# One block instead of separate stages: layers 2 and 3 of a three-layer decoder kernel, with parts of the out-projection, the next norm and the final rows put elsewhere

## Chip, cores and metric

One NeuronCore of one Trainium2 chip runs the whole kernel. The metric is the device time of one execution in microseconds (us); the figure for a kernel is the median of its runs. Engines: TensorE (PE), VectorE (DVE), ScalarE (ACT), GpSimd (POOL), and SyncE (SP), which here only issues DMAs.

## What is computed

256 tokens of width 1024 pass three layers in fp32. Layer 1 (RWKV, latent attention and 32 experts) is the same in both kernels. Layers 2 and 3 are, cut to what matters:

```python
for layer in range(2):
    h = rmsnorm(x, norm_mix[layer])
    if layer % 2 == 0:                       # "even": layer 2 of the kernel
        y = h @ ev_w_in                      # 1024 x 3048
        o_a = dsa_mixer(...)                 # 8 heads; keys picked per query: lax.top_k(score, 64)
        o_b = diff_mixer(...)                # 4 heads, two softmaxes each, a = p0 - lam * p1
        mix = concatenate([o_a, o_b]) @ ev_w_out
    else:                                    # "odd": layer 3 of the kernel
        y = h @ od_w_in                      # 1024 x 2608
        # nsa_mixer: compressed keys and values gelu(flat @ w1) @ w2, selected and windowed attention, gates
        mix = nsa_mixer(...) @ od_w_out
    x = x + mix
    x = x + (silu(g @ w_gate) * (g @ w_up)) @ w_down      # g = rmsnorm(x, norm_ffn[layer]), width 2816
return rmsnorm(x, norm_final)
```

## The kernel before

Rows of tokens lie in two row blocks of 128 (TT = 2), the width in 8 chunks of 128 (KC = 8). To keep fp32 accuracy, most matrix products are three fp16 products (high by high, low by high, high by low): ACT makes the high part of a weight tile (a copy to fp16), DVE the low part (what the copy left), and PE multiplies.

Layers 2 and 3 are six stages, each an `nc.Block` of its own. At a block's end every engine waits for all others. Inside a block each engine runs its own program in the order in which it is written, with semaphores between them:

- `even_in`: norm of x on DVE, 16 transposes (L341), the in-projection in 12 tiles of up to 256 columns (L358), and beside it rope, the index scores of the 8 picking heads, and `take_eight` eight times on DVE (L2906, L2907: the 8 largest scores of each row are found and struck out), then L2951 and L2952, which turn the struck-out scores into the mask `ev_chosen`.
- `even_attention`: 8 units, the four differential ones first. Of a unit, PE makes the scores (L3186 to L3202, for units 4 to 7 with the mask), DVE `smallest` (L3112, the smallest score of each row, since scores are negated), ACT the exponentials, DVE `weigh` (L3119 to L3129), PE the transposes (L3214), DVE and ACT a copy each, PE the product with the values (L3228, L3235).
- `out_swiglu` (L418), used by both layers: 96 products of 512 columns of the out-projection (L692; 48 for each row block), norm and transposes (L699) of the rows, then 11 blocks of the feed-forward part, each 96 products of 256 columns up (L723) and 24 of 512 columns down (L732), with the weights streamed by SP.
- `odd_in` (L3282): the norm of x once more, 16 transposes (L341), 10 tiles of in-projection (L358). Beside it POOL clears four tiles and issues five loads: `emb` (L3321), `w1s` in two loads of 1 MB (L3323) and `w2s` (L3324, L3325). PE transposes `emb` after tile 1 (L3450) once all five have landed. After tile 3 come 32 fp32 products of 65 columns (L3463), the compression.
- `sparse_attention`: 16 units of the same build, then `out_swiglu` again, with the final norm. Its last part: DVE adds the last products to x (L659), ACT squares, DVE makes the sum and the reciprocal (L665 to L667), ACT the root, DVE one product over the whole row block (L673), SP writes out 512 KB for each row block (L495).

Between layers 2 and 3 there is in addition the exit of `Held` (L176, L177), which sets semaphores back and joins all engines. PSUM and SBUF of a stage are freed at its end.

## Time and profile before

| | us |
|---|---|
| median of three runs | 1129.85 |
| the runs | 1123.79, 1129.85, 1134.23 |
| the profiled execution, of which the trace is | 1124.25 |
| its span, first to last instruction | 1122.1 |

| engine | busy us | share of the span | instructions |
|---|---|---|---|
| PE | 985.7 | 88% | 8661 |
| PE weight loads | 708.9 | 63% | 8661 |
| DVE | 596.0 | 53% | 958 |
| ACT | 470.7 | 42% | 795 |
| POOL | 104.6 | 9% | 111 |

Where the stages lie: layer 1 ends near 440; `even_in` to 526; `even_attention` to 568; its `out_swiglu` to 768; `odd_in` to 848; `sparse_attention` to 915; the last `out_swiglu` to the end. The granted clock of PE is given as a share of its full 2.4 GHz; 0.5 is the lower level of 1.2 GHz. A row of the timeline is: start, duration, engine, line, operation, what is written and read, how many instructions in a row, and in brackets the idle time before it with what ended it. A PE row's duration is that of the whole run of instructions.

### The profile page before, as it was taken

How to read it: one execution, taken by the hardware profiler on the slowest of the kernel's cores; microseconds unless marked ns; L12 is line 12 of the kernel's file. 1: busy time of each engine (PE TensorE's matmuls, PEld its weight loads, DVE VectorE, ACT ScalarE, POOL GpSimd, SP SyncE). 2: the span in 40 equal slices, each digit the busy share in tenths (PEclk: the TensorE clock that was granted, in tenths of full speed). 3: DMA queues.
4: the chain of work that ended last, by engine and by line, in shares of the span. 5: the costliest groups of instructions: out<-in, count | busy, mean ns of one | idle time of the engine just before them, and what ended most of it. 6: DMA issues, size and time to landing. Idle time of an engine off the chain costs nothing. (4 is left out here: it accounts for less than half of the span.)

```text
span 1122.1 us, 20430 instructions
## 1 busy us (share of the span) xinstructions
PE 985.7 (88%) x8661; PEld 708.9 (63%) x8661; DVE 596.0 (53%) x958; ACT 470.7 (42%) x795; POOL 104.6 (9%) x111
## 2 busy tenths in 40 slices
PE   6998899789666677997889999997998889999996
PEld 5675787445333343885548777774886547777773
DVE  5667588431000004798764554536886864645543
ACT  6456552310000004663555455424665655534532
POOL 3410360000000001025000000002040000000000
PEclk9999898889888999998899999998998999999998
DMA  8723005999999996662062755634842033666520
GB/s 279 242 89 128 2 3 201 423 397 420 421 421 421 421 414 226 230 224 94 21 225 77 249 183 179 211 112 133 265 139 76 1 118 128 225 224 222 187 77 38
DMA packets 108453, 228.58 MB, mean 204 GB/s; under 512 B 7273, under 2 KB 86171, under 8 KB 93787
## 3 DMA queue, kind: packets, MB, share of 16 engines
q1 hardware_dynamic: 105403, 219.38, 53.9%
q0 software_dynamic: 2976, 8.14, 2.5%
q8 instruction: 54, 0.88, 0.3%
q14 instruction: 20, 0.16, 0.0%
HBM read 224.63 MB, written 1.05 MB: 201 GB/s over the span
## 5 line engine op out<-in xcount | busy, mean ns | idle before, releaser
L584 DVE SCALAR_TENSOR_TENSOR ffn_wu_lo<-ffn_w_up,ffn_wu_hi 128x2048 f16<-128x2048 f32 x40 | 90.0, 2288 | 32.6 <-ACT ffn_wu_hi L500 32.4
L1180 PE MATMUL rw_pB<-ring,kept 128*32 128x256 f32 x864 | 71.9, 430 | 27.5 <-DMA ring<-in_w_up 21.3
L723 PE MATMUL ffn_pG<-ffn_hT_hi,ffn_wu_lo 128*128 128x256 f16 x320 | 87.2, 273 | 0.0
L723 PE MATMUL ffn_pG<-ffn_hT_hi,ffn_wu_hi 128*128 128x256 f16 x320 | 87.2, 273 | 0.0
L723 PE MATMUL ffn_pG<-ffn_hT_lo,ffn_wu_hi 128*128 128x256 f16 x320 | 87.2, 273 | 0.0
L723 PE MATMUL ffn_pU<-ffn_hT_hi,ffn_wu_hi 128*128 128x256 f16 x320 | 87.2, 273 | 0.0
L723 PE MATMUL ffn_pU<-ffn_hT_lo,ffn_wu_hi 128*128 128x256 f16 x320 | 87.2, 273 | 0.0
L723 PE MATMUL ffn_pU<-ffn_hT_hi,ffn_wu_lo 128*128 128x256 f16 x320 | 87.2, 273 | 0.0
L500 ACT ACTIVATE ffn_wu_hi<-ffn_w_up 128x2048 f16<-128x2048 f32 x40 | 74.2, 1900 | 13.5 <-DMA ffn_w_up<-in_ffn_w_up 9.0
L601 DVE SCALAR_TENSOR_TENSOR ffn_hidden<-ffn_pU,ffn_gated 128x512 f32<-128x512 f32 x22 | 15.2, 690 | 111.2 <-ACT ffn_gated L518 111.2
L1180 PEld LDWEIGHTS rw_pB<-ring,kept 128*32 128x32 f32 x864 | 38.9, 124 | 54.3 <-issue 41.8
L1113 DVE TENSOR_TENSOR rw_mu_a<-rw_pB,rw_mu_a 128x256 f32<-128x256 f32 x8 | 3.4, 424 | 129.0 <-PE rw_pB L1180 129.0
L271 DVE SCALAR_TENSOR_TENSOR in_w_lo<-wt,in_w_hi 128x2048 f16<-128x2048 f32 (+2 forms) x22 | 53.5, 2433 | 17.0 <-ACT in_w_hi L264 16.9
L584 DVE SCALAR_TENSOR_TENSOR ffn_wd_lo<-ffn_w_down,ffn_wd_hi 128x2048 f16<-128x2048 f32 x22 | 50.4, 2292 | 22.1 <-ACT ffn_wd_hi L500 22.1
L518 ACT ACTIVATE ffn_gated<-ffn_pG 128x512 f32<-128x512 f32 x22 | 13.1, 597 | 114.6 <-PE ffn_pU L723 114.5
L732 PE MATMUL ffn_pY<-ffn_wd_hi,ffn_h_hi 128*128 128x512 f16 x176 | 53.7, 379 | 0.6 <-DVE ffn_h_lo L584 0.6
L732 PE MATMUL ffn_pY<-ffn_wd_hi,ffn_h_lo 128*128 128x512 f16 x176 | 53.7, 379 | 0.0
L732 PE MATMUL ffn_pY<-ffn_wd_lo,ffn_h_hi 128*128 128x512 f16 x176 | 53.6, 379 | 0.0
L358 PE MATMUL in_pY<-in_w_hi,in_sT_hi 128*128 128x256 f16 (+2 forms) x352 | 44.6, 275 | 1.0 <-ACT in_sT_hi L297 0.3
L264 ACT ACTIVATE in_w_hi<-wt 128x2048 f16<-128x2048 f32 (+2 forms) x22 | 42.1, 1915 | 4.8 <-DMA wt<-in_ev_w_in 2.2
L358 PE MATMUL in_pY<-in_w_lo,in_sT_hi 128*128 128x256 f16 (+2 forms) x352 | 42.2, 273 | 1.1 <-DVE in_w_lo L271 1.1
L358 PE MATMUL in_pY<-in_w_hi,in_sT_lo 128*128 128x256 f16 (+2 forms) x352 | 42.7, 273 | 0.3
(660 smaller groups left out, 2183.4 us busy)
## 6 DMA issues: line engine op xcount, KB each, us to landing
ring<-in_w_gate SPq DMA_DIRECT2D x27, 1024.0 KB, 26.1
ring<-in_w_up SPq DMA_DIRECT2D x27, 1024.0 KB, 26.7
ring<-in_w_down SPq DMA_DIRECT2D x24, 1024.0 KB, 26.2
ffn_w_down<-in_ffn_w_down SPq DMA_DIRECT2D x22, 1024.0 KB, 5.0
ffn_w_up<-in_ffn_w_gate SPq DMA_DIRECT2D x20, 1024.0 KB, 7.6
ffn_w_up<-in_ffn_w_up SPq DMA_DIRECT2D x20, 1024.0 KB, 9.9
wt<-in_ev_w_in SPq DMA_DIRECT2D x9, 1024.0 KB, 5.6
wt<-in_od_w_in SPq DMA_DIRECT2D x9, 1024.0 KB, 6.4
```

The source lines that it names most:

```text
L264: self.nc.scalar.activation(self.w_hi[:, k % 2, :, 0:n], self.wt[:, k % 2, :, 0:n], ACT.Copy, scale=W_SCALE).then_inc(self.hi_ready, 1)
L271: self.nc.vector.scalar_tensor_tensor(self.w_lo[:, k % 2, :, 0:n], self.wt[:, k % 2, :, 0:n], W_SCALE, self.w_hi[:, k % 2, :, 0:n], ALU.mu ...
L358: ins = self.nc.tensor.matmul(self.pY[:, slot, t, 0:n], x[:, c, t * P:(t + 1) * P], w[:, slot, c, 0:n], start=(term == 0 and c == 0), stop ...
L500: copy = lambda o, i, scale=1.0: nc.scalar.activation(o, i, ACT.Copy, scale=scale)
L518: nc.scalar.activation(gated[:, s, :], pG[:, s, :], ACT.Silu, scale=1.0 / W_SCALE).then_inc(silu_done, 1)
L584: return nc.vector.scalar_tensor_tensor(out, whole, scale, hi, ALU.mult, ALU.subtract)
L601: nc.vector.scalar_tensor_tensor(into, pU[:, s, :], 1.0 / W_SCALE, gated[:, s, :], ALU.mult, ALU.mult).then_inc(hidden_ready, 1)
L723: ins = T.matmul(p[:, s, j * SEQ:(j + 1) * SEQ], w[:, s, m, c, j::NJ], h[:, c, :], start=(n == 0), stop=(n == 3 * KC - 1))
L732: return T.matmul(pY[:, t, half * 512:(half + 1) * 512], h[:, s, at:at + P], w[:, s, j, half * 512:(half + 1) * 512], start=False, stop=st ...
L1113: nc.vector.tensor_tensor(hidden[:], pU[:, 0:D_EXPERT], gated[:], ALU.mult).then_inc(hidden_ready, 1)
L1180: ins = nc.tensor.matmul(into[i * CAP:(i + 1) * CAP, 0:D_EXPERT], h[:, c, i * CAP:(i + 1) * CAP], held[:, c * D_EXPERT:(c + 1) * D_EXPERT] ...
```

## The change

Layer 1 stays. For layers 2 and 3 one SBUF tensor (`field`) and one PSUM tensor (`later_pB`) are cut by hand into the stages' tiles, so stages can overlap. Four stages (in-projection, attention, feed-forward, next in-projection) run in one block without a barrier between them, and the other two in a second one; the exit of `Held` now stands between `odd_in` and `sparse_attention`.

```diff
+                with nc.Block(no_gpsimd_drain=True) as block:
+                    @block.tensor
+                    def _(pe):
+                        in2.tensor(pe)
+                        ea.tensor(pe)
+                        ffn2.tensor(pe)
+                        in3.tensor(pe)
...
+            with Held(nc) as held, ExitStack() as ctx3:
...
+                    @block.tensor
+                    def _(pe):
+                        nsa.tensor(pe)
+                        ffn3.tensor(pe)
```

**Picking.** Three of the eight `take_eight` and the making of the mask go from the end of `even_in` into DVE's program of the attention, and PE waits for the mask before the first unit that needs it.

```diff
+EIGHTS = {8: 2, 9: 2, 10: 1, 11: 0}
...
         smallest(0)
+        take_eight(pick)
...
         smallest(1)
+        take_eight(pick)
         weigh(0)
...
             left(u)
+            if u == 0:
+                take_eight(pick)
+                choose(pick).then_inc(picked, 1)
+            if u in LATE_LOWS:
+                out.low_part(dve, LATE_LOWS[u])
...
         for u in range(units):
+            if u + 2 == 4:
+                pe.wait_ge(picked, 1)
```

DVE at the start of layer 2's attention, before (`ei_` and `ev_` are tiles of `even_in`, `ea_` those of the attention):

```order
L2951 TENSOR_SCALAR ei_score<-ei_score 128x384
L2952 TENSOR_TENSOR ev_chosen<-ei_score,con_causal 128x384
L2799 UNCONDITIONAL_BRANCH
L3103 UNCONDITIONAL_BRANCH
L3145 TENSOR_TENSOR ea_prod<-ev_lam 128x128
L3146 TENSOR_REDUCE ea_s<-ea_prod 128x2
L3112 TENSOR_REDUCE ea_low_max<-ea_pS 128x2 x2
L3149 TENSOR_TENSOR ea_neg<-ea_s 128x1
```

and now, where L3006 and L3007 are a `take_eight` and L3310 is `smallest`:

```order
L3343 TENSOR_TENSOR ea_prod<-field 128x128
L3344 TENSOR_REDUCE ea_s<-ea_prod 128x2
L3310 TENSOR_REDUCE ea_low_max<-later_pB 128x2 x2
L3006 MAX field<-field 128x8
L3007 MATCH_REPLACE field<-field 128x128
L3006 MAX field<-field 128x8
L3007 MATCH_REPLACE field<-field 128x256
L3349 TENSOR_TENSOR ea_neg<-ea_s 128x1
```

The branches at the block's end are gone, and the rounds stand behind the `smallest` of units 0 and 1 and the `left` of unit 0.

**Out-projection.** The 48 products of one row block are issued chunk by chunk from the attention's last units on, each chunk once its low part is there.

```diff
+        def project(c):
+            pe.wait_ge(low_out, min(c, units // 2) + 1)
+            project_first(c)
...
             if u == 7:
+                pe.wait_ge(out.low, KC)
+                project(0)
...
+        project(1)
         add_values(units - 1)
+        for c in range(2, KC):
+            project(c)
```

PE at the end of layer 2's attention, before:

```order
L3214 MATMUL ea_pT<-con_identity,ea_E 128x128 x6
L3258 MATMUL ea_pS<-con_identity,ea_st 128x128 x8
L3235 MATMUL ea_pO<-ea_ET,ev_v 64x256 x2
L3235 MATMUL ea_pO<-ea_ET,ev_v 64x128 x2
L3235 MATMUL ea_pO<-ea_ET,ev_v 64x256 x2
L3235 MATMUL ea_pO<-ea_ET,ev_v 64x128 x2
L3051 UNCONDITIONAL_BRANCH
L685 UNCONDITIONAL_BRANCH
L692 MATMUL ffn_pY<-even_wo_hi,evenT_hi 128x512
```

and now, with the out-projection at L862 and the transposes of the rows at L881:

```order
L3419 MATMUL later_pB<-con_identity,field 128x128 x6
L862 MATMUL later_pB<-field 128x512 x6
L3472 MATMUL later_pB<-con_identity,ea_st 128x128 x8
L3440 MATMUL later_pB<-field 64x256 x2
L3440 MATMUL later_pB<-field 64x128 x2
L862 MATMUL later_pB<-field 128x512 x6
L3440 MATMUL later_pB<-field 64x256 x2
L3440 MATMUL later_pB<-field 64x128 x2
L862 MATMUL later_pB<-field 128x512 x60
L881 MATMUL later_pB<-con_identity,mix 128x128 x8
L862 MATMUL later_pB<-field 128x512 x24
```

Twelve products of the out-projection stand inside the attention, 36 right behind it, and only the other row block's 48 are left around the transposes. Layer 3 does the same with its units 14 and 15.

**Next norm.** In layer 2 the last feed-forward block is multiplied row block by row block, the norm of a finished row block starts at once (sums on ACT, one `tensor_scalar` and a reciprocal on DVE instead of three operations), and the first two tiles of `odd_in` are multiplied row block by row block.

```diff
-                last_down(n_blocks - 1, (n_blocks - 1) % 2)
+        down_rows(1, 0)
...
+        last_rows(0, 0)
+        down_rows(1, 1)
+        if following:
+            following.turn(pe, 0)
+        last_rows(0, 1)
+        if following:
+            following.multiply_rows(pe, 0, 0).then_inc(following.rows_done, 1)
+            following.multiply_rows(pe, 1, 0, range(2))
+            following.turn(pe, 1)
+            following.multiply_rows(pe, 1, 0, range(2, 3)).then_inc(following.rows_done, 1)
+            following.multiply_rows(pe, 0, 1).then_inc(following.product, 1)
+            following.multiply_rows(pe, 1, 1).then_inc(following.product, 1)
```

**odd_in.** POOL's four memsets and five loads and SP's out-projection slices from the third on wait until the last products of the feed-forward part are done (`rest_free`), since their tiles lie where its tiles were. The compression products are put one by one between the products of tile 4.

```diff
     def gpsimd(pool):
         link = Link(pool, glink)
+        pool.wait_ge(*rest_free)
         nc.gpsimd.memset(hidK[:], 0.0)
...
-            pr.multiply(pe, k)
+            if k == 4:
+                pe.wait_ge(x_lower, 1)
+                pe.wait_ge(x_upper, 1)
+                pr.multiply(pe, k, compress)
+            elif k >= 2:
+                pr.multiply(pe, k)
             if k == 1:
                 pe.wait_ge(rows_in, 5 * 16)
```

PE at the change from layer 2 to layer 3, before:

```order
L732 MATMUL ffn_pY<-ffn_wd_hi,ffn_h_lo 128x512
L465 UNCONDITIONAL_BRANCH
L3430 UNCONDITIONAL_BRANCH
L341 MATMUL in_pT<-con_identity,in_xn 128x128 x16
L358 MATMUL in_pY<-in_w_hi,in_sT_hi 128x256 x16
```

and now (L915 is the down product, L430 the transposes, L461 the products of tiles 0 and 1, L3685 those of `emb`, L366 the later tiles):

```order
L915 MATMUL later_pB<-field 128x512 x36
L430 MATMUL later_pB<-con_identity,mix 128x128 x8
L915 MATMUL later_pB<-field 128x512 x12
L461 MATMUL later_pB<-field 128x256 x40
L430 MATMUL later_pB<-con_identity,mix 128x128 x8
L461 MATMUL later_pB<-field 128x256 x56
L3685 MATMUL later_pB<-con_identity,field 128x16 x2
L366 MATMUL later_pB<-field 128x256 x48
```

**Final rows.** Each half of a row block is multiplied by the norm's gain as soon as its sum is there, and by the root at the end, left half on ACT, right half on DVE; SP writes four pieces of 256 KB.

```diff
-                    nc.vector.scalar_tensor_tensor(x[:, t, :], x[:, t, :], end_st[:, 2, t:t + 1], end_row[:], ALU.mult,
-                                                   ALU.mult).then_inc(end_rows, 1)
+            nc.vector.tensor_tensor(xn[:, t, half_of(n)], x[:, t, half_of(n)], end_row[:, half_of(n)], ALU.mult)
...
+            nc.vector.tensor_scalar(x[:, t, 512:D], xn[:, t, 512:D], end_st[:, 2, t:t + 1], None, ALU.mult).then_inc(end_right, 1)
```

## Rows read from the trace of the kernel before

**Rows 1.** Windows: stretch, length, busy PE PEld DVE ACT POOL, clock, DMA share, GB/s

```profile
522.40:568.60 46.20, 33.10 (x220) 22.80 (x221) 31.80 (x94) 24.36 (x85) 0.00 (x0) 0.82 0.14 46
568.60:766.00 197.40, 197.05 (x1528) 142.02 (x1528) 99.71 (x86) 85.97 (x87) 0.00 (x0) 0.99 0.53 176
848.00:915.20 67.20, 57.32 (x452) 37.24 (x452) 51.52 (x162) 38.50 (x156) 0.00 (x0) 0.92 0.10 33
```

**Rows 2.** Waits of PE from 522 to 1122: total us, times, longest

```profile
PE in_pT L341 <- DVE in_xn L329: 7.1, 1, 7.1
PE ea_pS L3186 <- PEq L2799: 4.6, 1, 4.6
PE ffn_pY L692 <- PEq L3051: 3.3, 1, 3.3
PE ffn_pY L692 <- PEq L3519: 1.6, 1, 1.6
PE nsa_pS L3658 <- PEq L3309: 1.1, 1, 1.1
PE ffn_pG L699 <- ACT mix L500: 0.7, 1, 0.7
```

**Rows 3.** Timeline of DVE, the last picking rounds of `even_in`

```profile
522.04 0.29 DVE L2906 MAX8 ei_top<-ei_score 128x8 f32<-128x128 f32 x1
523.74 0.29 DVE L2906 MAX8 ei_top<-ei_score 128x8 f32<-128x128 f32 x1
525.83 0.56 DVE L2952 TENSOR_TENSOR ev_chosen<-ei_score,con_causal 128x384 bf16<-128x384 f32 x1
```

**Rows 4.** Timeline of DVE in layer 2's attention, and two windows

```profile
534.27 1.02 DVE L3112 TENSOR_REDUCE ea_low_max<-ea_pS 128x2 f32<-128x256 f32 x2
537.40 0.41 DVE L3112 TENSOR_REDUCE ea_low_max<-ea_pS 128x2 f32<-128x256 f32 x1
550.98 1.02 DVE L3112 TENSOR_REDUCE ea_low_max<-ea_pS 128x2 f32<-128x256 f32 x2 [0.88 <-PE ea_pS L3202]
...
525.40:535.60 10.20, 7.86 (x37) 4.13 (x37) 6.82 (x22) 5.19 (x20) 0.00 (x0) 0.50 0.64 207
541.00:552.70 11.70, 11.35 (x92) 7.59 (x90) 9.79 (x31) 7.01 (x31) 0.00 (x0) 1.00 0.00 0
```

**Rows 5.** Start of the out-projection: DVE's last low part, a window, down products

```profile
566.70 1.23 DVE L3173 TENSOR_TENSOR evenT_lo<-ea_dT,evenT_hi 128x1024 f16<-128x1024 f32 x1 [0.52 <-ACT evenT_hi L3101]
569.70:573.20 3.50, 3.50 (x10) 1.31 (x9) 2.97 (x2) 2.30 (x2) 0.00 (x0) 0.51 0.92 293
991.42 5.18 PE ffn_pY L732 x24
```

**Rows 6.** Layer 2 to layer 3: POOL and its last load, a window, PE

```profile
768.18 0.15 POOL L3317 MEMSET oi_hidK<- 128x64 f32 x1 [246.98 <-POOLq L177]
771.26 1.22 POOL L3323 DMA_DIRECT2D oi_w1s<-in_od_cmp_w  x1
779.04 1.15 POOL L3323 DMA_DIRECT2D oi_w1s<-in_od_cmp_w  x1 [6.57 <-issue]
780.73 0.71 POOL L3325 DMA_DIRECT2D oi_w2s<-in_od_cmp_w  x1
oi_w2s<-in_od_cmp_w POOLq DMA_DIRECT2D x1, 32.0 KB, 6.4
771.10:778.00 6.90, 4.95 (x22) 3.98 (x22) 5.08 (x6) 4.06 (x10) 1.37 (x2) 0.51 0.63 179
788.45 0.29 PE L3450 MATMUL in_pT<-con_identity,oi_emb 16*128 16x16 f32 x2
802.42 7.48 PE L3463 MATMUL in_pT<-oi_xp,oi_w1s 128*128 128x65 f32 x64 [0.92 <-DVE oi_xp L3406]
```

**Rows 7.** The end: DVE and SP's queue

```profile
1114.91 0.15 DVE L665 TENSOR_REDUCE ffn_end_st<-ffn_end_halves 128x1 f32<-128x2 f32 x1 [0.80 <-ACT mix L573]
1115.72 1.28 DVE L673 SCALAR_TENSOR_TENSOR x<-x,ffn_end_st,ffn_end_row 128x1024 f32<-128x1024 f32 x1 [0.27 <-ACT ffn_end_st L576]
```

2664 lines of the change are left out of this document (1432 added, 1232 removed).

## Prediction

> **What bounds the kernel now.** I read the windows by stage first. PE is busy for 197.05 of the 197.40 us of layer 2's out-projection and feed-forward part, at a granted clock of 0.99 [rows 1]: nothing is to be had there but fewer or faster products, and the change has neither. The same holds for the last feed-forward part, which ends the kernel. In layer 2's attention PE is busy for 33.10 of 46.20 us at a mean clock of 0.82, in layer 3's for 57.32 of 67.20 at 0.92 [rows 1]; DVE is the busiest other engine there (31.80 and 51.52). So the change can win what PE waits at the seams of the stages, what the clock loses behind such waits, and a little at the end. PE's waits after 522 [rows 2] name the seams: 7.1 us before the transposes of layer 3 (waiting for the norm's last row, DVE L329), 4.6 before layer 2's attention (the end of a block), 3.3 and 1.6 before the two out-projections (ends of blocks), 1.1 between `odd_in` and its attention, and 0.7 before the row transposes. All told 18.4 us, the ceiling of what waits alone can give. Behind the long ones the clock stands at half: 0.51 through 6.90 us after the 7.1 [rows 6], 0.51 through 3.50 us after the 3.3 [rows 5]. Half the clock for t of busy PE costs t/2: 3.4 and 1.7 us.
>
> **A, even_in to attention: 0.** PE's 4.6 us there go: PE needs the keys only, not the mask. But what ends the wait is DVE's picking. One `take_eight` takes 523.74 − 522.04 = 1.70 us, and the mask is done at 525.83 + 0.56 = 526.39 [rows 3]. Three rounds and the mask (two operations, 0.95 from the last round's end at 523.74 + 1.70) are now inside the attention, 5.1 + 0.95 = 6.05 us more on DVE. In the attention DVE sets the pace: from one `smallest` to the next are 537.40 − 534.27 = 3.13 us without idle time, and only at the last of them has it 0.88 free [rows 4]. So PE's first scores come 4.8 us earlier, DVE's fifth unit 6.05 − 4.8 = 1.2 us later; about 1.7 us of it is taken back where DVE waited for the first scores. I put down 0, with +1 and −2 as bounds; the two late low parts of the out-projection weights that DVE gets as well fill the 0.88 waits.
>
> **B, attention to out-projection in layer 2: +4.3.** The last low part ends at 566.70 + 1.23 = 567.93 [rows 5]. Chunks 0 and 1 are now inside the attention: 12 products of 5.18/24 = 0.216 us [rows 5], 2.6 us, which delay the chain behind them as much, so the last low part comes at 570.6. Chunks 2 and 3 (another 2.6 us) are issued while it is made. From there 24 products, 24 more, the transposes and 24 more remain. Counted the other way: the stretch from the last attention product to the first up product loses its 3.3 us wait [rows 2] and the 1.7 us of slow clock, 5.0 in all, and 0.7 stays for the chain. If one of the twelve runs at half clock the gain is 2.5 to 3.5; if nothing waits, 5.0, and with a faster transposition up to 5.5. Behind this wait stand on PE all of the feed-forward products; nothing else is late.
>
> **C, layer 2 to layer 3: +4.0.** Before, the transposes of `emb` come at 788.45 [rows 6]. Without the 7.1 us wait and the 3.4 us of slow clock that is 778.0; I add 1.0 for chunks that are waited for: 779.0. But the `emb` transposes wait for all of POOL's loads, and POOL now starts when the last products are summed, near 767, about a microsecond before it does now (768.18). Its first `w1s` is issued at 771.26, the second, after 6.57 us of idle, at 779.04, the last `w2s` at 780.73, which lands 6.4 us later, at 787.1 [rows 6]. From POOL's first memset to the last landing that is 18.9 us. Started at 766.9, it ends at 785.8 if nothing else changes. SP's loads of the next tile and of two slices of the output weights, which shared the DMA engines in this window (share 0.63 [rows 6]), are now issued earlier, so the two 1 MB loads should be quicker: I take 783.7, with 782.5 and 785.9 as bounds. So `emb` is transposed at 783.8 instead of 788.45, +4.65, after a new wait of 4.7 us. That wait will cost the clock what the others do: between 1.7 and 3.4, I take 2.5. Last, the 32 products of the compression, 64 instructions in 7.48 us [rows 6], are 0.117 us each for 65 columns, though 128x512 down products of fp16 need only 0.216; most of it is thus no streaming of columns, and between products of 256 columns it can be covered. I put +1.8, with 0 and +2.5 as bounds. 4.65 − 2.5 + 1.8 = 3.95. Bounds: with the late landing and the long slow clock −1; with no stall +11.
>
> Here a rule of the Trainium skill speaks for more. *DMA: Bandwidth & Descriptors*, section on the anatomy of one DMA of the gpsimd path, gives 2.0 us plus the bytes over 436e3 per us, so about 4.4 us for 1 MB; by it the two `w1s` would be through in under 9 us, all rows would land near 780, the stall would almost vanish and C be near +10. The trace disagrees: from one `w1s` to the next are 779.04 − 771.26 = 7.8 us. I go by the trace.
>
> **D, the exit of `Held` before layer 3's attention: −1.2.** It was covered by nothing either before, but it was inside the 7.1 us. POOL's row names it (L177) as what ended at 768.18, two us behind the feed-forward's last products at 766.0. Between `odd_in` and its attention the plain block's end costs 1.1 [rows 2]; with the exit I take 2.3. Bounds 0.5 and 2.
>
> **E, layer 3's attention to out-projection: +2.0.** The 1.6 us and the 0.7 us wait [rows 2] can go, 2.3 at most by waits, and 3 with better cover; 0.3 is left. Bounds 1 and 3.
>
> **F, the end: +1.5.** Before, after the last sum DVE waits 0.80 for ACT's squares, then three operations of 0.15, 0.27 for the root, then 1.28 for the whole row block [rows 7]: written by 1117.0. Also, DVE was still busy with the first row block when the last sums came (1 us late). Now the last operation is half a row block (0.64), one small operation is gone (0.15), and the first row block's work is in four short pieces: 0.64 + 0.15 + 1.0 = 1.8, less 0.3 for PE's last products, which end a little later since the norm of the first is fitted between. Bounds 1.2 and 2.6. What lies behind (the write and its completion) stays, with half the bytes in the last piece.
>
> **Sum.** 0 + 4.3 + 4.0 − 1.2 + 2.0 + 1.5 = 10.6 us. From the profiled execution of 1124.25 (span 1122.1 and 2.15 around it) that makes 1113.7. That execution was 5.6 below the median of the three runs; from the median 1129.85 it makes 1119.2, and I say **1119**.
>
> **Rivals.**
> - *The rows are there in time.* If the `w1s` loads, alone on their queue, take 5 us each, all is there by 779 to 780, C is about +11 and the sum 17.8: 1112. For it speaks that other loads went in the same window; against it that the second `w1s` followed the first only after 6.57 us of idle.
> - *The slow clock spreads into the attention (the other side).* PE now enters the attention 4.8 us early and is fed by a DVE that has 6 us more to do, so PE has gaps in every unit. Before, at full clock, units 4 to 7 took PE 11.35 of 11.70 us [rows 4]: PE-bound there. If the lower level, which before ended at 535.6 [rows 4], lasts through them, they cost 11.35 more, and the sum is 10.6 − 11.4 = −0.8: 1131, slower. It decides once the level stays low past the start of unit 4. For it: the clock was 0.50 for 10.2 us from 525.4 on, behind a wait of 4.6 us and with PE busy for 7.86 of it [rows 4], longer than behind the 7.1 us. Against it: it rose within the units before too, where PE was fed by the same DVE.
> - *The waits only move.* If the chain from the last unit to the chunks costs what the block's end did (B +2.5), C gives nothing (late landing, long slow clock: −1), A gives −0.5 and E +1.5, F +1.5, D −1.2, the sum is 2.8: 1127. For it speaks that each seam's barrier sat on a chain of data.
>
> **Chances.** The forecast 0.62, its own range 1115 to 1124; rows in time 0.15; waits only move 0.15; slow clock 0.08. The range of 1112 to 1128 leaves out 2 in 10. About 1% (11.3 us, or 1118.55) is what a measurement can tell from no change. The forecast lies 0.5 us above this: half of its chance (0.31) and all of the first rival's are faster, 0.46, and with a little of the rest 0.47; the other half, the moved waits and a little of the slow clock make 0.48 for within 1%; 0.05 for slower.
>
> **What would show it.** A: PE's first score near 522.2, and the fifth unit's `smallest` within 1 us of where it was. B: PE without idle time over 1 us from the last unit to the first up product, at clock 1.0. C: a wait of PE before the `emb` transposes of 3 to 6 us, released by POOL's DMA; if there is none, the first rival holds; if it is over 8, the third. Tile 4's products with compression in 12 to 13 us in all instead of 5.2 + 7.5. D: PE's wait before the second attention near 2.3. F: from PE's last product to the last issue of a write 3.0 to 3.5 us. My sum is wrong if stages that I take as unchanged (layer 1, the feed-forward loops) differ by over 1 us, or if the clock in the attention is low past unit 4.

## The result, and where the time went

| | before | changed |
|---|---|---|
| median of 20 runs, us | 1125.74 | 1118.99 |
| lowest to highest | 1120.06 to 1140.61 | 1116.24 to 1124.51 |
| profiled execution; its span | 1124.25; 1122.1 | 1122.0; 1120.2 |

The ratio is 0.9944 with a 95% interval of 0.9924 to 0.9964: 6.3 us faster, between 4.1 and 8.6 (the two medians lie 6.75 apart). It lies within 1% of no change. The prediction said 1119 and the median is 1118.99, but that agreement hides two errors. The forecast was 10.6 us taken off a median of three runs (1129.85); 20 runs put that median 4.1 us lower, and the gain is 6.3, not 10.6.

The two profiled spans differ by 1.9 us only, because the changed kernel's execution came out of layer 1 late: its first 96 products of layer 2's in-projection end at 458.60, those of before at 455.53, and nothing was changed ahead of that. I therefore measure every place from the end of these 96 products. Worked out from PE's rows of both traces in this way ("the prediction's" are its terms A to F, with + for time won):

| stretch, ended by | before | changed | gain | the prediction's |
|---|---|---|---|---|
| transposes of unit 6, layer 2's attention | 100.1 | 100.5 | -0.4 | A 0 |
| from there to the first up product | 36.3 | 31.7 | +4.6 | B +4.3 |
| feed-forward, to the last up product | 163.3 | 163.3 | 0 | 0 |
| to PE's wait before layer 3's attention | 91.8 | 93.1 | -1.3 | C +4.0 |
| that wait | 1.1 | 2.6 | -1.4 | D -1.2 |
| first scores to the values of unit 4 | 28.7 | 32.2 | -3.5 | not in it |
| to the first up product | 61.0 | 57.0 | +4.0 | E +2.0 |
| feed-forward, to the last product | 174.1 | 174.1 | 0 | 0 |
| last product to the end | 10.2 | 7.3 | +2.9 | F +1.5 |
| all | 666.6 | 661.6 | +5.0 | +10.6 |

The stretches at half clock between these 96 products and the last product add up to the same length in both traces, 37.6 us: six stretches before (10.24, 6.83, 3.41, 6.83, 6.83, 3.41), five after (3.41, 6.83, 6.83, 6.83, 13.65). They have moved between the places; single rows of the table hold up to 3.5 us of this.

The waits of PE in the changed kernel from 440 on (total us, times, longest), the answer to [rows 2]:

```profile
PE later_pB L3895 <- ACT field L3765: 7.6, 8, 2.0
PE later_pB L3685 <- DMA field<-in_od_cmp_w: 6.2, 1, 6.2
PE later_pB L3419 <- DVE field L3325: 3.6, 1, 3.6
PE later_pB L3704 <- DVE field L3643: 3.5, 1, 3.5
PE later_pB L3419 <- ACT field L3273: 3.1, 1, 3.1
PE later_pB L3878 <- PEq L178: 2.6, 1, 2.6
...
PE later_pB L3394 <- DVE field L3011: 0.7, 1, 0.7
```

Of before's seam waits, the 7.1 us one, the 4.6, the 3.3, the 1.6 and the 0.7 are gone. In their place stand a wait of 6.2 us for POOL's loads (L3685, the `emb` transposes), 3.6 before unit 0's transposes for VectorE's `weigh` (L3325), 3.5 before the query transposes (0.6 before the change), and 2.6 at the exit of `Held` (L178). The mask (L3011) costs PE 0.7.

Windows of the changed kernel (columns as in [rows 1]): the attention of layer 2, the stretch behind it up to the first up product, and the two slow stretches that matter:

```profile
524.70:559.00 34.30, 23.64 (x160) 14.88 (x160) 29.31 (x91) 19.22 (x76) 0.00 (x0) 0.85 0.29 89
559.00:590.70 31.70, 31.64 (x164) 17.80 (x165) 17.09 (x29) 17.02 (x29) 0.00 (x0) 0.89 0.32 113
782.10:789.00 6.90, 4.31 (x21) 3.13 (x22) 6.55 (x6) 3.24 (x6) 0.00 (x0) 0.51 1.01 336
850.40:864.10 13.70, 13.70 (x68) 10.47 (x64) 7.06 (x20) 4.46 (x20) 0.00 (x0) 0.50 0.98 307
```

In the first window VectorE is busy for 29.31 of 34.30 us and PE for 23.64. In the second PE is busy for 31.64 of 31.70: the seam between attention and out-projection has no idle time left. In the last PE works for 13.70 us without a pause at half its clock, where the trace of before has 6.8 us of it:

```profile
853.10:859.90 6.80, 6.80 (x34) 5.26 (x35) 5.46 (x17) 2.40 (x13) 0.00 (x0) 0.50 0.44 138
```

Twice as long at half the clock is 6.9/2 = 3.4 us, which is the 3.5 us of the table.

### The profile page after: what moved, and what is told of

Its sections match the earlier page's. It is cut to its first block and busy times, and to the rows that moved or that the text cites. A ratio compares the mean times of both kernels' runs of the same rounds, so it can differ in the third digit from the quotient of the medians.

```text
span 1120.2 us, 20400 instructions
## 1 busy us (share of the span) xinstructions
PE 990.3 (88%) x8661; PEld 711.3 (64%) x8661; DVE 594.6 (53%) x963; ACT 477.1 (43%) x817; POOL 104.5 (9%) x111
## 5 line engine op out<-in xcount | busy, mean ns | idle before, releaser
L906 PE MATMUL later_pB<-field 128*128 128x256 f16 x1920 | 212.9, 273 | 0.0
L906 PEld LDWEIGHTS later_pB<-field 128*128 128x128 f16 x1920 | 187.7, 98 | 25.6
L735 DVE SCALAR_TENSOR_TENSOR field<-field 128x2048 f16<-128x2048 f32 x84 | 153.9, 1869 | 55.4 <-ACT field L630 55.4
L630 ACT ACTIVATE field<-field 128x2048 f16<-128x2048 f32 x84 | 126.4, 1567 | 14.1 <-DMA field<-in_ffn_w_up 7.9
L366 PE MATMUL later_pB<-field 128*128 128x256 f16 (+2 forms) x960 | 118.3, 279 | 1.3 <-issue 0.4
L915 PE MATMUL later_pB<-field 128*128 128x512 f16 x528 | 117.7, 379 | 0.6 <-DVE field L735 0.6
L366 PEld LDWEIGHTS later_pB<-field 128*128 128x128 f16 x960 | 95.9, 100 | 16.2 <-ACT field L305 1.8
L1383 PE MATMUL rw_pB<-ring,kept 128*32 128x256 f32 x864 | 72.6, 434 | 26.8 <-DMA ring<-in_w_up 22.5
L915 PEld LDWEIGHTS later_pB<-field 128*128 128x128 f16 x528 | 51.6, 98 | 58.8 <-issue 1.5
L279 DVE SCALAR_TENSOR_TENSOR field<-wt,field 128x2048 f16<-128x2048 f32 (+2 forms) x22 | 53.3, 2430 | 24.2 <-ACT field L272 24.0
L272 ACT ACTIVATE field<-wt 128x2048 f16<-128x2048 f32 (+2 forms) x22 | 42.0, 1914 | 9.8 <-PEq L158 4.0
L862 PE MATMUL later_pB<-field 128*128 128x512 f16 x192 | 44.0, 384 | 0.0
L1404 PE MATMUL rw_pB<-ring,rw_mu_a 128*32 128x512 f32 x216 | 31.0, 629 | 8.8 <-DMA ring<-in_w_down 5.9
L366 PE MATMUL in_pY<-ring 128*128 128x256 f16 (+1 forms) x288 | 35.8, 279 | 0.8 <-ACT ring L272 0.7
```

What stands on the lines that cost most here:

```text
L272: self.nc.scalar.activation(self.w_hi[:, k % 2, :, 0:n], self.wt[:, k % 2, :, 0:n], ACT.Copy, scale=W_SCALE).then_inc(self.hi_ready, 1)
L279: self.nc.vector.scalar_tensor_tensor(self.w_lo[:, k % 2, :, 0:n], self.wt[:, k % 2, :, 0:n], W_SCALE, self.w_hi[:, k % 2, :, 0:n], ALU.mu ...
L366: ins = self.nc.tensor.matmul(self.pY[:, slot, t, 0:n], x[:, c, t * P:(t + 1) * P], w[:, slot, c, 0:n], start=(term == 0 and c == 0), stop ...
L630: copy = lambda o, i, scale=1.0: nc.scalar.activation(o, i, ACT.Copy, scale=scale)
L735: return nc.vector.scalar_tensor_tensor(out, whole, scale, hi, ALU.mult, ALU.subtract)
L862: return nc.tensor.matmul(pY[:, t, half_of(n)], source[:, c, t * P:(t + 1) * P], by[:, c, half_of(n)], start=(c == 0 and term == 0), stop= ...
```

## Experiments

All times at places count from the end of layer 2's first 96 in-projection products, as above. For the totals, ratios are to the kernel before, timed beside each; with 6 to 10 runs their intervals are 0.3 to 0.5% (3 to 5 us) to either side, so most single edits can't be told apart by their totals. The places can, within limits: between the two profiles of the changed kernel they differ by 0.7 us at most (next paragraph), but the nine traces of kernels that have the same instructions up to unit 6 (the changed kernel and all but e4, e6, e10 and e11) put it between 99.8 and 102.2, with the clock at half for 6.83, 10.24 or 13.65 us ahead of it. So a shift of 1 to 3 us counts only where the clock's stretches are the same. The columns are starts: of unit 6's transposes and the first up product in layer 2, of the `emb` and the query transposes, of the first scores, the values of unit 4 and the first up product in layer 3.

| kernel | unit 6 | up L2 | emb | query turns | scores L3 | unit 4 | up L3 | last product | end | median, ratio |
|---|---|---|---|---|---|---|---|---|---|---|
| before | 100.1 | 136.4 | 332.9 | 376.3 | 392.6 | 421.3 | 482.3 | 656.4 | 666.6 | 1 |
| changed | 100.5 | 132.1 | 326.1 | 373.3 | 391.0 | 423.2 | 480.2 | 654.3 | 661.6 | 1118.99, 0.9944 |
| e12_changed_again | 99.8 | 131.4 | 325.6 | 372.9 | 390.6 | 422.8 | 479.8 | 653.8 | 661.2 | 1119.23, 0.9942 |
| e1_early_w1 | 100.6 | 132.2 | 319.9 | 367.4 | 386.8 | 420.2 | 477.2 | 651.3 | 658.6 | 1115.58, 0.9934 |
| e2_compress_apart | 102.2 | 133.8 | 328.0 | 372.3 | 390.0 | 423.2 | 481.8 | 655.9 | 663.2 | 1117.26, 0.9940 |
| e3_early_apart | 99.8 | 131.4 | 319.1 | 370.4 | 388.1 | 418.2 | 476.8 | 650.9 | 658.2 | 1115.25, 0.9935 |
| e4_pick_back | 97.0 | 128.7 | 322.6 | 369.7 | 389.0 | 416.8 | 473.8 | 647.9 | 655.2 | 1115.46, 0.9917 |
| e5_no_exit | 99.8 | 131.4 | 325.5 | 372.7 | 389.0 | 417.8 | 476.4 | 650.5 | 659.1 | 1118.63, 0.9952 |
| e6_early_pick | 96.9 | 128.5 | 316.2 | 363.7 | 383.1 | 415.0 | 473.6 | 647.6 | 655.0 | 1114.24, 0.9907 |
| e7_project_after | 99.8 | 131.0 | 324.8 | 372.5 | 390.2 | 422.1 | 480.7 | 654.8 | 662.1 | 1120.59, 0.9968 |
| e8_two_writes | 100.3 | 131.9 | 326.2 | 373.5 | 391.2 | 423.4 | 480.3 | 654.4 | 661.7 | 1119.82, 0.9960 |
| e9_sparse_after | 100.5 | 132.1 | 326.2 | 373.4 | 392.8 | 420.5 | 477.3 | 651.4 | 658.8 | 1119.74, 0.9931 |
| e10_all_four | 97.0 | 128.6 | 316.3 | 367.5 | 383.8 | 413.2 | 470.2 | 644.3 | 652.9 | 1111.03, 0.9844 |
| e11_three | 96.8 | 128.4 | 316.1 | 364.9 | 383.9 | 411.6 | 470.2 | 644.3 | 652.9 | 1109.57, 0.9840 |

**The changed kernel a second time.** No edit.

> The changed kernel itself, profiled once more, to see what of its trace returns. In its first profile the slow clock at the start of the second attention lasted 13.65 us, in the kernels with one edit elsewhere 3.41 to 17.07 us. Theory 1, it belongs to the changed kernel (the wait of 2.6 us there): 13.65 again, and 32.2 us from the first score to the values of unit 4. Theory 2, it is drawn anew in each execution: another length, and that stretch between 27.5 and 33 us. The waits at the seams (0 before the first out-projection, 6.2, 3.5, 2.6) return to within 0.2 us by both.

The waits came back (6.45 us for the 6.2, then 3.5 and 2.6), and so did the slow stretch at the start of the second attention:

```profile
847.90:861.60 13.70, 13.70 (x68) 10.49 (x64) 7.06 (x20) 4.48 (x20) 0.00 (x0) 0.50 0.97 307
```

From the first score to the values of unit 4 are 32.2 us again. Theory 1 holds for these two profiles, and e8 has 13.65 and 32.2 too. But e9, whose edit lies behind this place, has the same instructions up to here and the same 2.6 us wait, and only 3.41 us of half clock, with 27.7 us to the values of unit 4. The window of 13.70 us that is slow throughout in the changed kernel is this one in e9 (it starts as far behind the first scores):

```profile
856.90:870.60 13.70, 12.44 (x96) 9.00 (x93) 11.46 (x34) 8.35 (x37) 0.00 (x0) 0.88 0.97 307
```

Of the four traces with the same instructions up to here three have 13.65 (theory 1) and one has not (theory 2): the wait belongs to the kernel, but the length of the stretch differs from one execution to another. In kernels with an edit ahead of the place it is 3.41 to 17.07 us.

**A, the picking rounds.**

```diff
-EIGHTS = {8: 2, 9: 2, 10: 1, 11: 0}
+EIGHTS = {8: 2, 9: 2, 10: 2, 11: 2}
...
                 take_eight(link)
+        link(choose(link))
...
         smallest(0)
-        take_eight(pick)
...
         smallest(1)
-        take_eight(pick)
...
-                take_eight(pick)
-                choose(pick).then_inc(picked, 1)
+                dve.sem_inc(picked, 1)
```

> The changed kernel, but all eight picking rounds and the mask stand on VectorE at the end of the in-projection again; everything else is as in the changed kernel. Theory 1, VectorE sets the attention's pace, so that what PE gains by starting early is given back: PE's first scores 0 to 1 us later (VectorE's rounds do not stop them), the attention ends within 1 us of the changed kernel's, the time is the same within 1 us. Theory 2, the rounds are hidden in the attention: this is 4 us slower.

Neither theory: it is faster. PE's first scores come at the same place (67.2), but unit 6 comes at 97.0 in place of 100.5, 3.5 us earlier. Of this 0.7 is the clock: here it is at half for 6.83 us ahead of unit 6, and the traces without this edit that have 6.83 too (e3, e5, e7, e12) put unit 6 at 99.8, 2.8 us later. At the end this profile is 6.4 us ahead of the changed kernel's; the rest is the clock's: 4.4 us less from layer 3's first scores to the values of unit 4 (3.41 us at half in place of 13.65), and 1.7 more behind the query transposes. VectorE in this kernel, end of the picking and first `smallest`:

```profile
529.08 0.56 DVE L3011 TENSOR_TENSOR field<-field,con_causal 128x384 bf16<-128x384 f32 x1
529.68 0.29 DVE L3344 TENSOR_TENSOR ea_prod<-field 128x128 f32<-128x128 f32 x1
530.00 0.29 DVE L3345 TENSOR_REDUCE ea_s<-ea_prod 128x2 f32<-128x128 f32 x1
530.21 1.01 DVE L3311 TENSOR_REDUCE ea_low_max<-later_pB 128x2 f32<-128x256 f32 x2
```

and in the changed kernel, where two rounds follow the first two `smallest`, and the third round and the mask come later:

```profile
527.72 1.02 DVE L3310 TENSOR_REDUCE ea_low_max<-later_pB 128x2 f32<-128x256 f32 x2 [5.23 <-PE later_pB L3400]
528.66 0.28 DVE L3006 MAX8 field<-field 128x8 f32<-128x128 f32 x1
...
540.09 0.36 DVE L3010 TENSOR_SCALAR field<-field 128x384 f32<-128x384 f32 x1
540.48 0.56 DVE L3011 TENSOR_TENSOR field<-field,con_causal 128x384 bf16<-128x384 f32 x1
```

The bracket is the point: in the changed kernel VectorE waited 5.23 us for PE's first scores with three rounds still to do. (In the changed kernel's second trace this wait is 4.55.) With the rounds ahead, that idle time takes them: this profile lies 2.42 us later (its 96 products end at 461.02, not 458.60), and 530.21 less 2.42 is 527.79, so the first `smallest` starts 0.07 us later than in the changed kernel, and the chain behind it has only its own work. Without barrier and with the rounds left where they were, unit 6 comes 3.1 us earlier than before the change (97.0 in place of 100.1); moving the rounds gave it back.

The 3.1 need not all be the barrier's. Before the change VectorE makes one more low part of the out-projection weights ahead of the picking,

```profile
504.39 2.28 DVE L399 SCALAR_TENSOR_TENSOR even_wo_lo<-ei_whole,even_wo_hi 128x1024 f16<-128x1024 f32 x1
529.21 1.02 DVE L3112 TENSOR_REDUCE ea_low_max<-ea_pS 128x2 f32<-128x256 f32 x2 [1.60 <-PE ea_pS L3195]
```

and the change moves it into the attention (`LATE_LOWS`), in e4_pick_back too. Its mask is therefore done 2.2 us earlier (68.6 in place of 70.9), and its first `smallest` comes at 69.2 in place of 73.7. No run takes the barrier away alone, so how the 3.1 us divide between the two stays open.

**B and E, the out-projection's place.** In layer 2 and, in the other kernel, in layer 3:

```diff
-                project(0)
...
-        project(1)
         add_values(units - 1)
-        for c in range(2, KC):
+        for c in range(KC):
             project(c)
```

> The changed kernel, but the chunks 0 and 1 of layer 2's out-projection are issued behind the last attention product and not between the last units. Theory 1 (the prediction's B): the 12 products inside delay the chain to the last low part as much as they take, so nothing is won by having them inside; outside, they fill the wait for that part: the first up product comes within 0.7 us of the changed kernel's. Theory 2, they fill idle time of the last units: 2.6 us slower.

From unit 6 to the first up product it takes 31.2 us against 31.7: theory 1. The products run straight on behind the attention without idle time (the second row is cut off by the window's end):

```profile
563.62 1.75 PE L3440 MATMUL later_pB<-field 128*64 128x256 f32 x16
565.30 1.90 PE L862 MATMUL later_pB<-field 128*128 128x512 f16 x8
```

So B's 4.6 us come from the missing barrier, from issuing chunk by chunk as the low parts arrive, and from a slow stretch that is gone (0.51 for 3.5 us before [rows 5]); that chunks 0 and 1 stand inside the attention is worth nothing. In all twelve other traces of kernels with the change this stretch is 31.6 to 31.7 us, so B's size is firm.

> The changed kernel, but in layer 3 all chunks of the out-projection's first row block are issued behind the last attention product, as e7_project_after does in layer 2. From the values of unit 13 to the first up product the changed kernel takes 24.5 us, the one before 29.5; the prediction's E has 2.0 of these 5.0. Theory 1, the gain is the barrier, its waits and the slow clock behind them, not the place of the chunks: 24.2 to 25.5 us here. Theory 2, the 18 products inside fill waits of the last units: 26 to 28.5 us here.

From the values of unit 13 to the first up product are 25.6 us, against 24.5 in the changed kernel and 29.5 before. But this measure was badly chosen: in the changed kernel chunk 0 stands ahead of unit 13's values, so its 1.5 us are not in the stretch. From the values of unit 4, which no chunk precedes in any of the three, it is 56.8 us here, 57.0 in the changed kernel and 61.0 before. Theory 1: the place of the chunks is worth nothing in layer 3 either, and E is the barrier, its waits and the clock. The clock's part is not the change's: behind a wait of 2.0 us that all 14 traces have in the last units, it fell for 3.41 us in seven (before, e2, e3, e5, e6, e7, e11) and not in the others. The same place before and in e7_project_after:

```profile
907.70:911.10 3.40, 3.40 (x19) 1.94 (x18) 1.25 (x5) 0.88 (x2) 0.00 (x0) 0.50 0.00 0
908.90:912.20 3.30, 3.30 (x12) 1.30 (x12) 1.29 (x5) 0.49 (x1) 0.00 (x0) 0.50 0.02 5
```

From the values of unit 4 to the first up product the kernels with the change take 58.6 us where it fell and 56.8 to 57.0 where it didn't. Like with like, E is 61.0 less 58.6, 2.4 us.

**C, the stall before the `emb` transposes.**

```diff
     def gpsimd(pool):
         link = Link(pool, glink)
+        pool.wait_ge(*weights_free)
+        for n in range(2):
+            nc.gpsimd.dma_start(w1s[:, n, :, :], w1[n].rearrange("(m p) e -> p m e", p=P)).then_inc(rows_in, 16)
         pool.wait_ge(*rest_free)
...
-        for n in range(2):
-            nc.gpsimd.dma_start(w1s[:, n, :, :], w1[n].rearrange("(m p) e -> p m e", p=P)).then_inc(rows_in, 16)
```

> The changed kernel, but POOL issues the two 1 MB loads of w1s as soon as the feed-forward's up weights are used up (weights_free, near 753 us) instead of after its last products. In the changed kernel PE waited 6.2 us for POOL's loads before the emb transposes, behind which came 1.5 us of slow clock; later it waited 3.5 us before the query transposes (0.6 before the change). Theory 1, the stall is on the path and the rest of the stage moves up with it: no wait before the emb transposes, 5 to 8 us less than the changed kernel. Theory 2, the second half of the stage is tied to a chain of its own (tile loads, low parts and ropes on DVE): the 3.5 us wait grows to 9 to 11, and under 2 us are won. Theory 3, loads in the last feed-forward blocks disturb its weight loads: PE gets new waits before 766.

The stall is gone and nothing in the feed-forward part moved (its last up product ends at 295.4, as in the changed kernel). PE in the changed kernel, and then in this one:

```profile
771.40 7.06 PE L461 MATMUL later_pB<-field 128*128 128x256 f16 x56
784.69 0.39 PE L3685 MATMUL later_pB<-con_identity,field 16*128 16x16 f32 x2 [6.23 <-DMA field<-in_od_cmp_w]
785.01 7.33 PE L366 MATMUL later_pB<-field 128*128 128x256 f16 x48
```

```profile
767.11 7.06 PE L461 MATMUL later_pB<-field 128*128 128x256 f16 x56
774.11 0.29 PE L3686 MATMUL later_pB<-con_identity,field 16*128 16x16 f32 x2
774.33 5.41 PE L366 MATMUL later_pB<-field 128*128 128x256 f16 x48
```

The 48 products behind it take 5.41 us in place of 7.33, the slow clock's share. Up to the query transposes 5.9 us are left of it, and up to the first scores of layer 3 4.3: the slow clock came back later, for 3.41 us in the tiles behind. So all of the 6.2 us are won at the `emb` transposes, but 3.0 at the end (3.4 by the medians), less than theory 1's 5 to 8. Theories 2 and 3 are out: the wait before the query transposes is 3.49 us as in the changed kernel, and PE has no new waits before the stage. POOL's rows show why the stall was there in the changed kernel:

```profile
766.38 0.15 POOL L3544 MEMSET field<- 128x64 f32 x1 [243.01 <-PE later_pB L915]
...
769.59 1.22 POOL L3550 DMA_DIRECT2D field<-in_od_cmp_w  x1
776.99 1.15 POOL L3550 DMA_DIRECT2D field<-in_od_cmp_w  x1 [6.18 <-issue]
...
778.68 0.71 POOL L3552 DMA_DIRECT2D field<-in_od_cmp_w  x1
```

From one `w1s` to the next are 7.4 us, and in e1_early_w1, with its idle time of 8.19 us before the second, 9.4: as in [rows 6], POOL issues the second only when the first has landed, 0.3 to 0.4 us behind its landing in each of these traces. The edit issues the first load at 729.7 in this trace, earlier than the 753 expected.

**C, the compression between the products of tile 4.**

```diff
-                pr.multiply(pe, k, compress)
+                for n in range(CMP_LEN):
+                    compress(n)
+                pr.multiply(pe, k)
```

> The changed kernel, but the 32 products of the compression stand as a piece before tile 4, as before the change. Theory 1, by the sum of the prediction: interleaving wins 1.8 us, so this is 1 to 2 us slower. Theory 2, by the trace after: interleaving shortens PE's work by 0.6 us only, but gives ScalarE its last compression product 4 us later (811.3 instead of about 807.3), and the chain from there to the query transposes ends the wait of 3.5 us; apart is then 0 to 2 us faster.

Theory 2. From the `emb` transposes to the query transposes it takes 44.3 us in place of 47.2, 2.9 less. The end doesn't show it: this profile had 1.7 us more of slow clock in layer 2's attention and more again in layer 3's (17.07 and 3.41 us at half in place of 13.65), and the medians (0.9940 and 0.9944) can't tell 2 us. Groups of PE's rows in the changed kernel from 800.7 to 811.5:

```profile
L3668 PE MATMUL later_pB<-field 128*128 128x65 f32 x64 | 10.7, 280 | 0.0
L366 PE MATMUL later_pB<-field 128*128 128x256 f16 x35 | 9.7, 287 | 0.0
```

and PE in e2_compress_apart:

```profile
804.43 7.47 PE L3668 MATMUL later_pB<-field 128*128 128x65 f32 x64 [0.47 <-DVE field L3629]
811.72 10.66 PE L366 MATMUL later_pB<-field 128*128 128x256 f16 x96
...
833.89 1.94 PE L3706 MATMUL later_pB<-con_identity,field 128*128 128x128 f32 x16 [0.63 <-DVE field L3643]
```

Interleaved, 32 pairs with 32 products take 0.333 us each (from 800.73 on, row by row), 10.7 in all; apart they take 7.47 + 32 x 0.111 = 11.0. So next to nothing was covered. But the last of the compression products came 26.8 us behind `emb` in place of 22.3, and on ScalarE everything waits for it in order: in the changed kernel

```profile
811.49 0.17 ACT L3561 ACTIVATE field<-later_pB 128x2 f32<-128x2 f32 x1 [9.72 <-PE later_pB L3668]
811.68 1.28 ACT L3591 ACT_TABLE_LOAD   x1
...
814.85 1.92 ACT L272 ACTIVATE field<-wt 128x2048 f16<-128x2048 f32 x1
```

ScalarE idles 9.72 us, and the high part of tile 6 follows at 814.85; from its low part at 816.80 on, VectorE works with no pause longer than 0.21 us to the operation (L3643) that releases the query transposes at 831.93.

**Both edits of C together.**

> Both edits of the two kernels before. If the stall and the compression's place are two causes in a row, the gains add up: the first one's plus 0 to 2 us. If the second half is tied to the tile loads, it is no better than the better one of the two.

They don't add up: by the end (658.2; e1 has 658.6) it is no better than the better one of the two, though not because of the tile loads. The wait before the query transposes is 0.6 as in e2, but they come at 370.4, later than in e1 (367.4). The clock was at half for 13.65 us, from within the compression's products on. e10_all_four shows the same at the same place; its PE rows and the window:

```profile
787.47 12.48 PE L3667 MATMUL later_pB<-field 128*128 128x65 f32 x64 [2.09 <-DVE field L3628]
...
789.00:802.70 13.70, 13.70 (x67) 12.80 (x66) 6.98 (x11) 4.60 (x6) 0.00 (x0) 0.50 0.51 166
```

Behind a wait of 2.1 us the clock fell and stayed down while these fp32 products of 65 columns ran, 12.48 us in place of 7.47. In e1, e6 and e11, where a wait of 2.05 us is followed by these products with others of 256 columns among them, the clock didn't fall (e1, e6) or was down for 3.41 us (e11). Two traces against three suggest that interleaving has a benefit once the stall is gone; they don't show it, since the same code also gave 13.65 and 3.41 us elsewhere (e12, e9).

**D, the exit of `Held`.** Both blocks share one set of semaphores, and POOL clears those of the first stages inside the first block:

```diff
+        with Held(nc) as held, ExitStack() as later:
...
                         in3_pool(pool)
+                        nc.clear_and_free_semaphores(early_sems)
```

> The changed kernel without the exit of Held between odd_in and the second attention: both blocks share one set of semaphores (GpSimd clears those of the in-projection and the first attention inside the first block), and only the block's own end stands between them. In the changed kernel PE waits 2.6 us there, before the change 1.1. Theory 1, the exit costs what the wait shows: the wait falls to 1.1 to 1.3 and the end comes 1.4 us earlier, the clock behind it unchanged. Theory 2, the longer wait is also what keeps the clock low longer in the first units of the second attention (13.65 us against 6.83 before): then another 3 us come back.

```profile
PE later_pB L3878 <- PEq L4089: 1.1, 1, 1.1
```

The wait fell from 2.6 to 1.1, and the slow stretch behind it from 13.65 to 10.24 us (28.8 us to the values of unit 4 in place of 32.2); another 3.41 came in the last units. The last product comes 3.8 us earlier than in the changed kernel's first profile (0.6 of this lies ahead of the `emb` transposes, where nothing was changed), but the end only 2.5: the one exit that is left clears more semaphores (0.85 us in place of 0.33 for the clear itself), and the last write landed 0.6 us later. The 1.4 us of theory 1 are seen at the place (the first scores start 16.25 us behind the query transposes in place of 17.68); the total (0.9952, where the changed kernel has 0.9944) confirms neither theory. That the shorter wait causes the shorter slow stretch I can't say: e9 and e4 have the 2.6 us wait and only 3.41 us of slow clock behind it. It stays open.

**F, the writes.**

```diff
-                for n, scaled in enumerate((end_left, end_right)):
+                for scaled in (end_left, end_right):
                     sp.wait_ge(scaled, t + 1)
-                    sp.dma_start(last[1][:, t, half_of(n)], x[:, t, half_of(n)]).then_inc(stored, 16)
+                sp.dma_start(last[1][:, t, :], x[:, t, :]).then_inc(stored, 16)
```

> The changed kernel, but SP writes two pieces of 512 KB, each when both halves are scaled, in place of four of 256 KB. From the last product to the end the changed kernel takes 7.3 us, the one before 10.2. Theory 1, the smaller last piece is worth 1 us (in the changed kernel 3.6 us lie between SP's last issue and the end, before it 4.7): 8.3 us here. Theory 2, the gain at the end is all in VectorE's and ScalarE's shorter last steps: 7.3 to 7.6 us.

7.3 us from the last product to the end, as in the changed kernel: theory 2. The smaller piece lands 0.4 us sooner (1.9 us behind the end of its issue against 2.3), and the additional issue costs as much. VectorE at the end of the changed kernel, the answer to [rows 7]:

```profile
1112.93 0.69 DVE L798 SCALAR_TENSOR_TENSOR x<-later_pB,x 128x512 f32<-128x512 f32 x1
1113.65 0.69 DVE L803 TENSOR_TENSOR mix<-x,field 128x512 f32<-128x512 f32 x1
1114.41 0.21 DVE L808 TENSOR_SCALAR ffn_end_st<-ffn_end_halves 128x1 f32<-128x1 f32 x1
1114.65 0.16 DVE L809 RECIPROCAL ffn_end_st<-ffn_end_st 128x1 f32<-128x1 f32 x1
1115.09 0.49 DVE L811 TENSOR_SCALAR x<-mix,ffn_end_st 128x512 f32<-128x512 f32 x1 [0.27 <-ACT ffn_end_st L725]
```

The last sum ends at 1113.6, 0.8 us behind the last product at 1112.85 (before, the last sums ended 2.2 us behind it, since the first row block's work stood in front of them), and the last scaling is 0.49 us here and 0.72 for ScalarE's half, in place of 1.28. From the last product to the last issue of a write it is 3.4 us, within the 3.0 to 3.5 that the prediction named.

**Together.** e6 joins the early loads and the rounds put back; e11 adds the missing exit; e10 takes the compression apart as well.

> The changed kernel with two edits together: the w1s loads early, and all picking rounds back in the in-projection. Measured from the first products of layer 2, each alone moved the last product by 3.0 and 6.4 us; at the places themselves they won 6.2 us (the stall before the emb transposes) and 3.5 us (the units of the first attention), the rest came from where the clock fell. If they add up at their places, the last product comes about 9 to 10 us earlier than in the changed kernel, less or more 3.4 us for the clock, and the time is 1110 to 1114. If both were luck of the clock, it is within 3 us of the changed kernel.

> The same without the third of them: the compression stays between the products of tile 4. By e6_early_pick (6.6 us earlier at the end than the changed kernel) and e5_no_exit (1.4 at its place) it is 8 to 9 us below the changed kernel, and within 2 us of e10_all_four.

> The changed kernel with four edits together: w1s loads early, compression apart, picking rounds back in the in-projection, no exit of Held between odd_in and the second attention. If each keeps at its place what it gave alone (6.2 before the emb transposes, 2.9 before the query transposes, 3.5 in the first attention, 1.4 before the second), it is 10 to 14 us below the changed kernel; if the early loads take away the reason for the 2.9 (as in e3_early_apart), 8 to 11.

e6: 9.9 us ahead of the changed kernel at the `emb` transposes, 9.6 at the query transposes, 8.0 at the first scores of layer 3, 6.6 at its first up product and at the end: the two edits add up at their places, and slow stretches behind take a third of it. The median of 1114.24 is just outside the 1110 to 1114 expected. e11: the last product at 644.3, 9.9 us earlier, and 0.9840 of the kernel before (0.9792 to 0.9889): 1109.57 us, faster than both kernels; e10 is the same within its interval (0.9799 to 0.9890): 8.7 us below the changed kernel at the end, the second of its two cases (8 to 11), and 8.0 by the medians. The compression's place makes no difference any more in these two traces: PE's wait before the query transposes falls from 3.49 to 0.63, but they come later (367.5; e11 has 364.9), by the clock.

## Why the prediction was right and where it was wrong

- **What bounds the kernel**: right. The two feed-forward stretches took 163.3 and 174.1 us in both kernels.
- **A**: the size was right (0 forecast, -0.4 measured, +0.3 by the second profile), and for the reason given: VectorE sets the pace and got 6.05 us more; its fifth `smallest` comes at 85.5 in place of 85.4. What the prediction did not see is that VectorE's idle wait of 5.23 us for the first scores was the place for the rounds. It took the barrier's removal and the moving of the rounds as one edit; apart they are +3.1 and -3.5 (-2.8 with the clock's stretches alike). It counted the two late low parts as work in the attention, and not that one of them had stood ahead of the picking.
- **B**: right in size (4.3 forecast, 4.6 measured) and mechanism, though its sign of a clock at 1.0 from the last unit on did not come: 6.83 us at half lie there in both kernels (0.89 over the stretch). e7 confirms that the twelve products inside gain nothing by themselves.
- **C**: wrong, 4.0 forecast and -1.3 measured, and with it the sum. By place, `emb` is transposed 2.6 us earlier behind the last up product where 4.65 was forecast, and from there to the query transposes it takes 47.2 us in place of 43.4. Three terms. The stall was foreseen with its cause (4.7 us; it was 6.2, as POOL's loads landed 18.3 us behind its first memset in place of the 17 that I chose from bounds of 16 to 19). The slow clock behind it was sized right (2.5; 1.9 by the 48 products). The compression failed: I counted +1.8 for covering what is not streaming of columns, and it was -2.9 (e2). The premise that 65 columns are short and the rest can be covered was an argument from a single price; the run shows 0.333 us for a pair and a product, which is nearly the sum of both (0.345), so 0.3 us were covered in all. The sign given for it could not have told: 12 to 13 us for tile 4 with the compression is what 5.2 + 7.5 = 12.7 give without any cover, and +1.8 would have been 10.9; it measured 10.7 + 16 x 0.111 = 12.4. And I did not ask who waits for the last of these products; the head start of 2.5 us was given back there.
- **D**: right (-1.2; -1.4 measured).
- **E**: the mechanism was right, the size was not: 4.0 in place of 2.0. I summed the waits (1.6 + 0.7 = 2.3) and left out the slow stretch that lay in the last units before, 3.41 us from 907.69 on at 0.50, and is not in the changed kernel's two traces: 1.7 us. But it stands in six of the other eleven traces with the change, e7's among them. Where it is in both, the gain is 2.4 us, so the 2.0 was sized well and the other 1.7 is what the two profiles happened to have. e9 shows that the chunks' place adds nothing.
- **F**: 2.9 in place of 1.5. By the scaled rows 1.7; the rest lies behind the last issue: the write lands 0.4 us sooner, and from there to the end it is 1.7 us in place of 2.5, of which the clear at the last exit of `Held`, with fewer semaphores, is 0.24 (0.33 us in place of 0.57); I had taken both as unchanged.
- **Not in the sum**: the slow clock at the start of layer 3's attention, 13.65 us in place of 6.83, 3.5 us of loss. D named a longer wait there, but I priced the wait without its clock, though I had done so at B and C. How much of the loss is the change's stays open: e9, with the same instructions up to there, has 3.41 us, and there is one trace of before.
- **The rivals**: the forecast's case is what happened in B and D, the third rival's (what C wins is given back) in C. The slow clock did not spread through the units of layer 2's attention (units 4 and 5 ran at the full clock); it struck in layer 3's, for 3.5 us and not 11.
- **The base**: three runs of the kernel before were 4.1 us higher in the median than 20. The predicted time of 1119 was hit by luck: this error and the one of the gain cancelled. From the profiled execution the prediction's sum gave 1113.7, and the changed kernel's profiled execution took 1122.0. Of the stages taken as unchanged the feed-forward loops are the same to 0.1 us; layer 1 differs by 3.1, over the 1 us that the prediction named as a sign of being wrong, but nothing was changed in it, and the end of the first 96 products behind it varies between 453.5 and 463.3 over the 14 traces.

## What to carry to other kernels

When a barrier goes, look at each engine's idle time on its far side before moving work: the engine that ends the wait may have room ahead of the barrier, and the next chain has none (A). Work moved between other instructions to be hidden must be followed to whoever waits for its last part, on engines that issue in order above all (C). Price every new wait with the clock it can cost behind it, and a wait that goes with the clock it gives back: here this was from nothing to 6.8 us behind a single wait. It differs between executions of the same code, so compare places only between traces whose slow stretches are alike, and take more than one trace.

## What the runs showed of the hardware

- What a wait costs in PE's granted clock differs between executions. Behind one wait of 2.0 us in layer 3's last units, the same in all 14 traces, the clock fell to half in seven, for 3.41 us; behind the 3.5 us wait before the query transposes, in ten traces, it fell in five (e1, e4, e6, e9, e11), for 3.41 us or 6.83 (e11); behind the 2.6 us wait before layer 3's attention the same instructions ran 13.65 us at half (changed, e8, e12) or 3.41 (e9).
- Behind a wait of 2.1 us the clock was at half for 13.65 us in the two traces in which 64 fp32 products of 65 columns followed alone (e3, e10), and for 3.41 us or not at all in the three in which fp16 products of 256 columns stood among them (e11; e1, e6). That what ran is the cause is not shown.
- Two loads of 1 MB issued by GpSimd one behind the other don't overlap: 7.3 to 9.6 us lie between their issues in all 14 traces, the second is issued 0.3 to 0.4 us after the first has landed, and GpSimd is idle for 6.1 to 8.4 us before it. Where two small loads (64 and 32 KB) stand right behind the second, they are issued without such a wait. The Trainium skill, *DMA: Bandwidth & Descriptors*, section on the anatomy of one DMA of the gpsimd path, has a formula that makes about 4.4 us for such a load, an estimate; the trace doesn't agree, with 6.8 us to landing as the median in the changed kernel, where other loads ran beside them.
- Small fp32 products (32, each of two instructions with 65 columns) between fp16 products of 256 columns cost nearly what they cost alone: 0.333 us for the group against 0.234 + 0.111.
